# Expert weights read with two neighbouring matrix rows per partition in a two-layer hybrid trunk

## The chip, the cores and the metric

The kernel runs on one core of one Trainium2 chip. The core has a matrix engine (TensorE, PE in the profile, with its weight loads shown apart as PEld), a vector engine (VectorE, DVE), an engine for pointwise functions (ScalarE, ACT), GpSimd (POOL) and SyncE (SP). They run independently and wait for each other on semaphores. Data moves between the device's memory (HBM) and the on-chip memory (SBUF) through 16 DMA engines, which all queues share. The metric is device time in microseconds for the whole program, the median of the runs. All arithmetic is in 32-bit floats.

## What is computed

Two layers over 256 latent tokens and 256 context tokens, model width 1024. A layer is: modulation by a conditioning vector, three attention mixers with gates and an output projection, layer norm; then modulation again, a mixture of 16 experts in which each expert chooses its 32 tokens, and layer norm. The second layer leaves out the context tokens behind its attention, since only the latent stream is returned. What the change touches is the expert part:

```python
h = x * (1.0 + sc2) + sh2                   # modulation, one scale and shift per channel
y = expert_choice_ffn(h, w_router[l], w_gate[l], w_up[l], w_down[l])
x = layer_norm(ALPHA * x + g2 * y, ln2_g[l], ln2_b[l])

def expert_choice_ffn(h, w_router, w_gate, w_up, w_down):
    aff = jax.nn.softmax((h @ w_router).astype(jnp.float32), axis=-1)
    top_aff, top_idx = lax.top_k(jnp.swapaxes(aff, 1, 2), cap)          # cap = 32
    xs = h[bidx, flat].reshape(b, N_EXPERTS, cap, d)
    hid = jax.nn.silu(jnp.einsum('becd,edf->becf', xs, w_gate)) * jnp.einsum('becd,edf->becf', xs, w_up)
    ys = jnp.einsum('becf,efd->becd', hid, w_down) * top_aff[..., None].astype(h.dtype)
    return jnp.zeros_like(h).at[bidx, flat].add(ys.reshape(b, N_EXPERTS * cap, d))
```

`w_gate`, `w_up` and `w_down` are 1024 by 1024 matrices, one of each per expert and layer: 12 MB per expert, 192 MB per layer. They are read once, and each is used by 64 tokens in the first layer (32 of each stream) and by 32 in the second.

## The kernel before

The program is written out by hand, one instruction list per engine, and nothing reorders it. In each layer come: the input projection and attention (`qkv`, `attention`), the gates (`gates`), the output projection with the router (`project_and_route`), the choice of tokens (`choose`) and the experts (`experts`).

**How weights come in.** All weights of the program pass through one ring of 8 slots of 1 MB (`ring`, 128 partitions of 2048 floats each). The list `stream` holds them in the order in which PE uses them; SP goes through it and issues the load of piece n once the matmuls on piece n-8 are done (lines 836 to 868). So at most 8 pieces are on their way or waiting. The first four pieces of each layer's first expert have places of their own in `A` and `B` (`early_piece`) and are loaded once the gates are done. The modulation weights `w_ada` go through the same ring, as pieces of 128 rows of 2048 floats.

**How an expert matrix is cut.** `into(e)` takes `w_gate` and `w_up` in four pieces each, in turn, and `down(e)` takes `w_down` in four. A piece (number `kp`) is 256 rows of the matrix, 1 MB that lie together in HBM. It is loaded with the source view `"(k p) n -> p k n"`: partition p receives row 256 kp + p and row 256 kp + 128 + p, two runs of 4 KB. The matmul with contraction tile k then needs the 128 channels 128 k to 128 k + 127 of the tokens on its partitions.

**Who supplies the channels.** For gate and up, `gather(l, part)` on PE multiplies `X[:, tile, k * P:(k + 1) * P]` (128 channels as the stationary operand) with the one-hot choice of 4 experts; there are four such parts, part 0 ahead of the experts (in `choose`) and the others in `experts` behind `into(1)`, `into(2)` and `into(3)`. ACT (`gathered`) takes each result from PSUM into `xsT` and applies scale and shift there, from columns of `modcol`, one column for each 128 channels. For down, `turn_hidden(e)` transposes the columns `j * P:(j + 1) * P` of `hid`.

**An expert on PE**: `into(e)`; for e = 1 to 3 a gather; for e = 5, 9, 13 a scatter of four finished experts; `down(e - 1)`; `turn_hidden(e)`. With 64 tokens (first layer) a piece is four matmuls of 512 columns, with 32 tokens (second layer) eight of 256. The output rows of each expert are moved inside SBUF by four DMAs that POOL issues (`move_rows`, `B<-A` in the profile).

**The modulation columns.** `ada_rows(l)` transposes the finished `modcol` of a layer into a spare PSUM bank, ACT copies it to `mod_rows`, and POOL stores it. Its place in the first layer is in the attention, for the second layer in the first layer's experts (`ada_due`).

Of the kernel before, what the change touches and what calls it, by code (L numbers as in the profile page):

```python
# [17 lines left out]
P = 128  # L18
D = 1024
KT = D // P  # L20
DEPTH = 2
# [44 lines left out]
def trunk(nc, x, c, ctx_in, c_ctx, w_ada, b_ada, w_in, a_sink, b_q_norm, b_kv_norm, b_w_uq, b_w_ukv, c_q_norm,  # L66
          c_k_norm, w_branch, w_out, ln1_g, ln1_b, w_router, w_gate, w_up, w_down, ln2_g, ln2_b, consts, out):
    es = ExitStack()
    with es:
# [34 lines left out]
        bias_cols = sb("bias_cols", [P, 48 * DEPTH])  # L104
        modcol = sb("modcol", [P, DEPTH, 2, 48])
        mod_rows = sb("mod_rows", [96, P])
        wr = sb("wr", [P, KT, EXPERTS])
        sink = sb("sink", [P, HEADS_A])
        nsink = sb("nsink", [P, HEADS_A])
# [82 lines left out]
        bias_in = sem("bias_in")  # L192
        mod_stored = sem("mod_stored")
        mod_cols = sem("mod_cols")
        part_in = sem("part_in")
        parts = [0]
        early_in = [sem(f"early_in{i}") for i in range(4)]
# [57 lines left out]
        def second(eng, key):  # L255

            b, _, n = groups[key]
            eng.wait_ge(bank_drained[b], n - 1)
            return b

        def streams(l):
            return [0, 1] if l < DEPTH - 1 else [1]
# [87 lines left out]
        def _(pe):  # L350
# [84 lines left out]
            def ada_rows(l):  # L435
                pe.wait_ge(mod_cols, 3 * l + 3)
                b = begin(("adaR", l), bank=TURN_BANK)
                end(nc.tensor.transpose(psum[0:96, b, 0:P], modcol[:, l, :, :].rearrange("p s c -> p (s c)"), ident), b)

            def ada_hook(step):  # L440
# [256 lines left out]
            def gather(l, part):  # L697

                lo, w, per = gather_cut(l, part)
                for k0 in range(0, KT, per):  # L700
                    b = begin(("XS", l, part, k0))
                    at = 0
                    for k in range(k0, k0 + per):
                        for s in streams(l):
                            for i in (0, 1):
                                ins = mm(psum[:, b, at:at + w], X[:, 2 * s + i, k * P:(k + 1) * P],
                                         onehot[:, 2 * s + i, lo:lo + w], i == 0, i == 1)
                            at += w
                    end(ins, b)
# [16 lines left out]
            def experts(l):  # L726
# [4 lines left out]
                def into(e):  # L731
                    bg = begin(("HG", l, e))
                    bu = begin(("HU", l, e))
                    for part, (lo, _) in enumerate(GATHERS):
                        if e == lo:
                            for k0 in range(0, KT, gather_cut(l, part)[2]):
                                drained(pe, ("XS", l, part, k0))
                    for kp in range(4):
                        for at, (b, w) in enumerate(((bg, w_gate), (bu, w_up))):
                            src = [w[l, e, kp * 256:kp * 256 + 256, :]]  # L740
                            if e == 0 and kp < 2:
                                n, v = None, early_piece(l, 2 * kp + at, src, 2, D)
                            else:
                                n, v = piece(src, 2, D)
                            for k in (2 * kp, 2 * kp + 1):
                                for g in range(G):
                                    ins = mm(psum[g * M:(g + 1) * M, b, 0:Wd], xsT[:, k, e * M:(e + 1) * M],
                                             v[:, k % 2, g * Wd:(g + 1) * Wd], k == 0, k == KT - 1)
                            if kp == 3:
                                free(n, event=end(ins, b))  # L750
                            elif n is not None:
                                free(n, ins)

                def turn_hidden(e):
                    pe.wait_ge(hid_ready, EXPERTS * l + e + 1)
                    transposes(("HT", l, e), [hid[:, e % 2, j * P:(j + 1) * P] for j in range(Wd // P)])

                def down(e):
                    drained(pe, ("HT", l, e))
                    b = begin(("YE", l, e))  # L760
                    for kp in range(4):
                        n, v = piece([w_down[l, e, kp * 256:kp * 256 + 256, :]], 2, D)
                        for k in (2 * kp, 2 * kp + 1):
                            q, j = k // (Wd // P), k % (Wd // P)
                            for g in range(G):
# [69 lines left out]
        def _(sp):  # L835
            sp.dma_start(cst[:, :], consts).then_inc(consts_in, 16)

            for dst, src, n, after in stream:
                if after:

                    sp.wait_ge(*after)
                    sp.dma_start(dst, src[0].rearrange("(k p) n -> p k n", p=P)).then_inc(early_in[n], 16)
                    continue
                if n >= RING:
                    sp.wait_ge(*freed[n - RING])
# [95 lines left out]
        def _(act):  # L941
# [27 lines left out]
            def ada_hook(step):  # L969
# [3 lines left out]
                if "rows" in due:  # L973
                    b = filled(act, ("adaR", due["rows"]))
                    if due["rows"]:

                        act.wait_ge(mod_stored, 16 * due["rows"])
                    nc.scalar.copy(mod_rows[:, :], psum[0:96, b, 0:P]).then_inc(bank_drained[b], 1)

            def modulated(name, l, t, scale, shift, halves=(0,)):  # L980
# [146 lines left out]
            for l in range(DEPTH):  # L1127
# [43 lines left out]
                def gathered(part):  # L1171
                    lo, w, per = gather_cut(l, part)
                    n = len(streams(l))
                    for k0 in range(0, KT, per):
                        b = filled(act, ("XS", l, part, k0))
                        at = 0
                        for k in range(k0, k0 + per):
                            dst = xsT[:, k, n * lo:n * (lo + w)].rearrange("p (e m) -> p e m", m=M)
                            for i, s in enumerate(streams(l)):
                                ins = nc.scalar.activation(dst[:, :, CAP * i:CAP * i + CAP],  # L1180
                                                           psum[:, b, at:at + w].rearrange("p (e m) -> p e m", m=CAP),
                                                           ACT.Identity,
                                                           scale=modcol[:, l, s, 8 * SC2 + k:8 * SC2 + k + 1],
                                                           bias=modcol[:, l, s, 8 * SH2 + k:8 * SH2 + k + 1])
                                at += w
                        ins.then_inc(bank_drained[b], 1)

                if l == 0:
                    ada_hook("routed")
                gathered(0)  # L1190
                Wd = D * M // P
                for e in range(EXPERTS):
# [471 lines left out]
```

## Time and profile before

| | us |
|---|---|
| Median of 3 runs | 1913.62 (1913.56 to 1915.73) |
| Span of the profiled execution | 1912.5 |
| PE busy | 1559.2 (82%) |
| PE weight loads busy | 783.9 (41%) |
| DVE / ACT / POOL busy | 495.3 / 389.5 / 84.9 |
| Moved by DMA | 529.01 MB, mean 277 GB/s |

Times of the profile count from the span's start. The 40 slices of the page are 47.8 us each. The experts are on the engines from about 559 to 1090 us (first layer) and from about 1397 us to the end (second layer). The busy share of the DMA engines counts the time in which they held a packet, and can come out a little over 1. "SPq" is the time of SP's DMA-issuing instructions. A matmul of 32-bit floats stands in the profile as two records.

### The profile page before, as it was taken

What the parts mean: (1) busy time and instruction counts of PE and PEld (TensorE: products, weight loads), DVE (VectorE), ACT (ScalarE), POOL (GpSimd) and SP (SyncE); (2) the same over time, 40 slices, a digit from 0 to 9 for tenths busy, and PEclk for the clock granted to TensorE, in tenths of its full rate; (3) what the DMA queues carried; (4) which work ended last, traced back from release to release, by engine and by line L of the source; (5) the groups of instructions that cost most, each with busy time, mean ns of one, the idle gap of its engine ahead of it and who ended that gap; (6) DMA issues with size and microseconds to landing.
All of it is one profiled execution on the core that took longest, in us unless ns stands there. A gap on an engine that the chain in (4) does not pass through costs nothing.

```text
span 1912.5 us, 21336 instructions
## 1 busy us (share of the span) xinstructions
PE 1559.2 (82%) x8780; PEld 783.9 (41%) x8780; DVE 495.3 (26%) x1063; ACT 389.5 (20%) x877; POOL 84.9 (4%) x169
## 2 busy tenths in 40 slices
PE   5999999999979988778787799999866666666664
PEld 1544457888544522122222264578542322222221
DVE  0125775333440001010010344865320000000002
ACT  1313674222122200000000132753220000000000
POOL 1000000000000000000000010000000000000000
PEclk8999999999989999999999999999987767676767
DMA  9445713225258999999999721056769999999994
GB/s 377 154 171 245 289 40 99 98 86 186 109 204 340 396 394 400 393 403 392 403 400 391 275 65 39 1 159 214 286 238 401 406 402 405 402 406 402 406 402 184
DMA packets 151408, 529.01 MB, mean 277 GB/s; under 512 B 12800, under 2 KB 15120, under 8 KB 145168
## 3 DMA queue, kind: packets, MB, share of 16 engines
q1 hardware_dynamic: 143536, 510.44, 69.4%
q0 software_dynamic: 7232, 16.76, 2.8%
q8 instruction: 70, 1.15, 0.2%
q10 hardware_dynamic: 544, 0.45, 0.1%
q14 instruction: 26, 0.21, 0.0%
HBM read 520.17 MB, written 1.15 MB: 273 GB/s over the span
## 4 chain that ended last, share of the span: by engine, by line
PE 52%; DMA 37%; DVE 6%; SPq 4%; ACT 1%; issue 1%; ACTq 0%; POOL 0%; DVEq 0%
PE psum L412 48%; DMA ring<-in_w_up 17%; DMA ring<-in_w_down 15%; SPq L850 4%; PE psum L458 3%; DMA ring<-in_w_gate 2%; DMA ring<-in_w_in 2%; DVE small L1418 1%; DMA ring<-in_w_ada 1%; DVE PR L1438 1%; DVE X L1450 0%; DVE X L1449 0%; ACT hT L987 0%; DVE psum L1416 0%; DVE stats L1539 0%
## 5 line engine op out<-in xcount | busy, mean ns | idle before, releaser
L412 PE MATMUL psum<-ring,A 128*32 128x256 f32 (+2 forms) x4704 | 721.1, 547 | 254.6 <-DMA ring<-in_w_up 87.4
L412 PEld LDWEIGHTS psum<-ring,A 128*32 128x32 f32 (+2 forms) x4704 | 235.2, 139 | 713.4 <-issue 280.1
L412 PE MATMUL psum<-ring_r,h_hi 128*128 128x512 f32 x576 | 179.9, 394 | 5.8 <-DVE h_lo L1592 5.8
L1552 DVE TENSOR_TENSOR A<-A,psum 128x512 f32<-128x512 f32 (+1 forms) x32 | 17.7, 554 | 625.4 <-PE psum L412 625.4
L412 PE MATMUL psum<-ring,hT 128*128 128x512 f32 (+2 forms) x512 | 170.2, 486 | 10.7 <-DMA ring<-in_w_in 5.3
L412 PEld LDWEIGHTS psum<-ring_r,h_hi 128*128 128x128 f32 x576 | 109.5, 190 | 29.5 <-issue 6.6
L1199 ACT ACTIVATE A<-psum 128x512 f32<-128x512 f32 (+1 forms) x32 | 15.7, 491 | 519.0 <-PE psum L412 519.0
L412 PEld LDWEIGHTS psum<-ring,hT 128*128 128x128 f32 x512 | 85.6, 192 | 82.0 <-issue 79.2
L412 PE MATMUL psum<-ring_r,h_lo 128*128 128x512 f32 x288 | 113.1, 393 | 0.0
L346 POOL DMA_DIRECT2D B<-A x120 | 58.9, 497 | 951.2 <-DVE A L1568 950.2
L1592 DVE TENSOR_TENSOR ring_r<-ring,ring_r 128x2048 fp32r<-128x2048 f32 (+2 forms) x36 | 73.7, 2053 | 93.2 <-ACT ring_r L1118 93.0
L412 PE MATMUL psum<-A 128*128 128x512 f32 (+5 forms) x240 | 93.6, 526 | 3.6 <-ACT A L1180 3.6
L1568 DVE TENSOR_TENSOR A<-psum,PR 128x512 f32<-128x512 f32 (+1 forms) x32 | 17.9, 558 | 301.5 <-PE psum L412 301.5
L1118 ACT CAST ring_r<-ring 128x2048 fp32r<-128x2048 f32 (+2 forms) x36 | 61.9, 1719 | 133.8 <-DMA ring<-in_w_in 108.4
L1210 ACT COPY A<-psum 128x512 f32<-128x512 f32 (+1 forms) x32 | 15.4, 481 | 352.6 <-PE psum L458 352.6
L412 PE MATMUL psum<-ring,cs 128*32 128x512 f32 x384 | 54.9, 651 | 13.4 <-DMA ring<-in_w_ada 12.6
L1418 DVE TENSOR_REDUCE small<-psum 128x1 f32<-128x512 f32 (+1 forms) x96 | 57.4, 598 | 23.2 <-PE psum L412 22.2
L1083 ACT ACTIVATE PR<-psum,small 128x512 f32<-128x512 f32 (+1 forms) x96 | 58.7, 612 | 20.8 <-PE psum L412 7.1
L458 PEld LDWEIGHTS psum<-cst,PR 128*128 128x128 f32 x320 | 38.4, 142 | 52.3 <-DVE PR L1438 25.6
L412 PEld LDWEIGHTS psum<-ring_r,h_lo 128*128 128x128 f32 x288 | 54.8, 190 | 11.4
L412 PE MATMUL psum<-ring_r,o_hi 128*128 128x512 f32 x192 | 59.1, 389 | 0.0
L412 PE MATMUL psum<-B,hT 128*128 128x512 f32 x96 | 49.2, 667 | 9.6 <-DMA B<-A 9.6
(168 smaller groups left out, 1202.9 us busy)
## 6 DMA issues: line engine op xcount, KB each, us to landing
ring<-in_w_down SPq DMA_DIRECT2D x128, 1024.0 KB, 18.5
ring<-in_w_gate SPq DMA_DIRECT2D x124, 1024.0 KB, 18.7
ring<-in_w_up SPq DMA_DIRECT2D x124, 1024.0 KB, 19.1
ring<-in_w_ada SPq DMA_DIRECT2D x48, 1024.0 KB, 9.9
ring<-in_w_in SPq DMA_DIRECT2D x36, 1024.0 KB, 5.0
ring<-in_w_out SPq DMA_DIRECT2D x8, 1024.0 KB, 6.2
ring<-in_w_branch SPq DMA_DIRECT2D x8, 768.0 KB, 4.4
B<-A POOLq DMA_DIRECT2D x60, 64.0 KB, 5.8
```

The lines of the kernel that those rows point to most:

```text
L346: eng.dma_start(YG[CAP * (e % 4):CAP * (e % 4) + CAP, 2 * (g % 2) + s, n * Wd:(n + 1) * Wd], ysb[at:at + CAP, e % 2, 0:Wd]).then_inc(signa ...
L412: return nc.tensor.matmul(o, a, b, start=start, stop=stop, skip_group_check=True)
L458: ins = nc.tensor.transpose(psum[0:rows, b, i * P:(i + 1) * P], s, ident)
L850: sp.dma_start(dst, src[0].rearrange("(k p) n -> p k n", p=P)).then_inc(slot_filled[n % RING], 16)
L1083: nc.scalar.activation(prob[:, u % 4, 0:nk * P], psum[:, b, 0:nk * P], ACT.Exp, bias=small[:, c4:c4 + 1], scale=SCALE_B if br == "B" else ...
L1118: nc.scalar.copy(hi, src).then_inc(split_high, 1)
L1199: nc.scalar.activation(sil[:, e % 2, 0:Wd], psum[:, b, 0:Wd], ACT.Silu).then_inc(bank_drained[b], 1)
L1418: run(V_.tensor_reduce(small[:, c4 + 3:c4 + 4], psum[:, b, 0:nk * P], AX, ALU.max, negate=True))
L1438: V_.tensor_scalar(prob[:, u % 4, 0:nk * P], prob[:, u % 4, 0:nk * P], small[:, c4 + 2:c4 + 3], None, ALU.mult).then_inc(prob_ready, 1)
L1552: V_.tensor_tensor(hid[:, e % 2, 0:Wd], sil[:, e % 2, 0:Wd], psum[:, b, 0:Wd], ALU.mult) \
L1568: V_.tensor_tensor(ysb[:, (e - 1) % 2, 0:Wd], psum[:, b, 0:Wd], gate_y[:, 0:Wd], ALU.mult) \
L1592: V_.tensor_tensor(lo, src, hi_read, ALU.subtract).then_inc(split_low, 1)
```

## The change

A piece of an expert matrix is still the same 1 MB, but its source view is now `"(p j) n -> p j n"` with j = 2: partition p receives rows 256 kp + 2p and 256 kp + 2p + 1, which are neighbours in HBM. Both sides of the DMA are then one run of 8 KB per partition, 128 in all where there were 256 of 4 KB. Contraction tile k = 2 kp + j now stands for the 128 channels 256 kp + j, 256 kp + j + 2, and so on. To match, the stationary operand of the gather and that of the transposes of `hid` are read with a step of two floats (`pair_cols`), and the scale and shift columns that ACT applies must be in the permuted order: PE picks them out of `modcol` with four small matmuls per layer in `ada_rows`, ACT copies them to a new tile `modpair`, and `gathered` reads that.

```diff
+        modpair = sb("modpair", [P, DEPTH, 2, 2, KT])
+        def row_pairs(m):
+            return m.rearrange("(p j) n -> p j n", j=2)
+        def pair_cols(k):
+            return slice(256 * (k // 2) + k % 2, 256 * (k // 2) + 256, 2)
...
             def ada_rows(l):
                 pe.wait_ge(mod_cols, 3 * l + 3)
                 b = begin(("adaR", l), bank=TURN_BANK)
+                for j in (0, 1):
+                    for h in (0, 1):
+                        mm(psum[64 * h:64 * h + 64, b, P + j:P + 32:2], ident[:, j::2],
+                           modcol[:, l, :, 8 * SH2 + h:8 * SC2 + 8:2])
...
-                                ins = mm(psum[:, b, at:at + w], X[:, 2 * s + i, k * P:(k + 1) * P],
+                                ins = mm(psum[:, b, at:at + w], X[:, 2 * s + i, pair_cols(k)],
...
-                            src = [w[l, e, kp * 256:kp * 256 + 256, :]]
+                            src = row_pairs(w[l, e, kp * 256:kp * 256 + 256, :])
...
-                    transposes(("HT", l, e), [hid[:, e % 2, j * P:(j + 1) * P] for j in range(Wd // P)])
+                    transposes(("HT", l, e), [hid[:, e % 2, pair_cols(j)] for j in range(Wd // P)])
...
-                        n, v = piece([w_down[l, e, kp * 256:kp * 256 + 256, :]], 2, D)
+                        n, v = piece(row_pairs(w_down[l, e, kp * 256:kp * 256 + 256, :]), 2, D)
...
-                    sp.dma_start(dst, src[0].rearrange("(k p) n -> p k n", p=P)).then_inc(early_in[n], 16)
+                    sp.dma_start(dst, src).then_inc(early_in[n], 16)
...
+                    nc.scalar.copy(modpair[:, due["rows"], :, :, :],
+                                   psum[:, b, P:P + 32].rearrange("p (s w k) -> p s w k", s=2, w=2)) \
+                        .then_inc(modpair_ready, 1)
                     nc.scalar.copy(mod_rows[:, :], psum[0:96, b, 0:P]).then_inc(bank_drained[b], 1)
...
-                                                           scale=modcol[:, l, s, 8 * SC2 + k:8 * SC2 + k + 1],
-                                                           bias=modcol[:, l, s, 8 * SH2 + k:8 * SH2 + k + 1])
+                                                           scale=modpair[:, l, s, 1, k:k + 1],
+                                                           bias=modpair[:, l, s, 0, k:k + 1])
...
+                act.wait_ge(modpair_ready, l + 1)
                 gathered(0)
```

No instruction changes its place against the others. What is new on an engine's list stands at three places. On SP, where the first layer's expert loads begin (the shape is partitions by runs by floats; `in_w_ada` is a modulation piece), before:

```order
L847 DMA ring<-in_w_ada 128x2048 x4
L842 DMA A<-in_w_gate 128x2x1024
L842 DMA A<-in_w_up 128x2x1024
L842 DMA B<-in_w_gate 128x2x1024
L842 DMA B<-in_w_up 128x2x1024
L850 DMA ring<-in_w_gate 128x2x1024
```

and now:

```order
L861 DMA ring<-in_w_ada 128x2048 x4
L856 DMA A<-in_w_gate 128x2048
L856 DMA A<-in_w_up 128x2048
L856 DMA B<-in_w_gate 128x2048
L856 DMA B<-in_w_up 128x2048
L861 DMA ring<-in_w_gate 128x2048
```

The order is the same; an expert piece now has the form that a modulation piece had already, and so it is for all 384.

On PE, where `ada_rows(0)` stands in the first layer's attention (`modcol` are the modulation columns, `cst` the identity), before:

```order
L412 MATMUL psum<-A 128x256
L412 MATMUL psum<-ring,cs 32x512 x4
L412 MATMUL psum<-A 128x256
L438 MATMUL psum<-cst,modcol 96x128
L458 MATMUL psum<-cst,PR 128x128 x2
L412 MATMUL psum<-A 128x256
```

and now:

```order
L422 MATMUL psum<-A 128x256
L422 MATMUL psum<-ring,cs 32x512 x4
L422 MATMUL psum<-A 128x256
L422 MATMUL psum<-modcol,cst 64x16 x4
L452 MATMUL psum<-cst,modcol 96x128
L472 MATMUL psum<-cst,PR 128x128 x2
```

Four matmuls of 16 columns come in ahead of the transpose that was there.

On ACT at the same place, before:

```order
L1081 ACTIVATE small<-sink,small 128x1
L1083 ACTIVATE PR,small<-psum,small 128x256
L978 COPY mod_rows<-psum 96x128
L1097 COPY W<-psum 128x2x128
L1081 ACTIVATE small<-sink,small 128x1
```

and now:

```order
L1098 ACTIVATE small<-sink,small 128x1
L1100 ACTIVATE PR,small<-psum,small 128x256
L992 COPY modpair<-psum 128x32
L995 COPY mod_rows<-psum 96x128
L1114 COPY W<-psum 128x2x128
L1098 ACTIVATE small<-sink,small 128x1
```

One copy of 32 columns comes in ahead of the copy of `mod_rows`.

## Rows read from the trace of the kernel before

**Rows 1.** The page: GB/s moved in 40 slices; DMA packets by size
```profile
GB/s 377 154 171 245 289 40 99 98 86 186 109 204 340 396 394 400 393 403 392 403 400 391 275 65 39 1 159 214 286 238 401 406 402 405 402 406 402 406 402 184
DMA packets 151408, 529.01 MB, mean 277 GB/s; under 512 B 12800, under 2 KB 15120, under 8 KB 145168
```

**Rows 2.** Windows of both expert stretches: engines' busy us, clock, DMA share, GB/s
```profile
640.00:1070.00 430.00, 342.20 (x1461) 104.29 (x1457) 37.83 (x55) 22.16 (x44) 27.99 (x57) 1.00 1.03 397
1410.00:1890.00 480.00, 313.08 (x3127) 120.62 (x3116) 22.82 (x46) 22.13 (x58) 29.44 (x60) 0.72 1.01 398
```

**Rows 3.** Chain that ended last, first layer, then end: start, us, what
```profile
658.92 16.30 PE psum L412 x104
...
682.87 18.61 DMA ring<-in_w_down
...
1866.93 20.85 DMA ring<-in_w_down
```

**Rows 4.** PE's timeline at a second-layer expert: start, us, matmuls [idle before <-cause]
```profile
1605.00 1.94 PE L412 MATMUL psum<-ring,A 128*32 128x256 f32 x16 [0.62 <-DMA ring<-in_w_gate]
1607.57 1.93 PE L412 MATMUL psum<-ring,A 128*32 128x256 f32 x16 [0.63 <-DMA ring<-in_w_up]
1610.13 1.89 PE L412 MATMUL psum<-ring,A 128*32 128x256 f32 x16 [0.63 <-DMA ring<-in_w_gate]
```

**Rows 5.** Windows where the experts begin in the first layer, then in the second
```profile
565.00:570.00 5.00, 3.55 (x32) 3.36 (x31) 0.00 (x0) 4.42 (x12) 0.00 (x0) 1.00 0.03 13
...
575.00:580.00 5.00, 5.00 (x26) 2.07 (x24) 0.00 (x0) 0.00 (x0) 0.00 (x0) 1.00 0.00 0
580.00:585.00 5.00, 5.00 (x28) 2.15 (x24) 0.60 (x1) 0.67 (x2) 0.00 (x0) 1.00 0.93 315
...
1400.00:1405.00 5.00, 3.20 (x39) 2.80 (x41) 0.00 (x0) 4.25 (x9) 0.00 (x0) 0.98 0.00 0
```

**Rows 6.** Windows with 8 KB runs (modulation pieces), then with 4 KB runs (expert pieces)
```profile
142.00:154.00 12.00, 12.00 (x40) 5.23 (x39) 2.40 (x6) 1.81 (x5) 0.00 (x0) 1.00 1.00 421
192.00:206.00 14.00, 13.88 (x92) 7.01 (x92) 10.94 (x47) 10.32 (x39) 0.00 (x0) 1.00 1.01 420
...
625.00:635.00 10.00, 10.00 (x71) 6.62 (x68) 0.69 (x1) 3.51 (x9) 0.00 (x0) 1.00 1.03 412
1445.00:1455.00 10.00, 6.58 (x68) 2.14 (x64) 0.00 (x0) 0.38 (x1) 0.00 (x0) 0.68 1.03 410
```

**Rows 7.** DMA rate in 40 slices of 640 to 1070 us, then of 1410 to 1890 us
```profile
GB/s 395 389 408 379 400 410 380 409 410 373 402 409 371 410 410 374 410 409 383 407 409 400 381 409 371 409 407 383 410 408 370 410 410 399 380 409 372 407 410 373
```
```profile
GB/s 400 409 394 410 408 394 410 394 408 410 396 410 409 393 410 394 410 407 395 409 401 403 408 396 410 408 395 409 397 408 409 396 408 409 395 409 394 410 409 180
```

**Rows 8.** SP's issues as the first layer's expert loads begin: start, us of issuing
```profile
579.18 0.37 SPq L850 DMA_DIRECT2D ring<-in_w_gate  x1
...
600.56 0.37 SPq L850 DMA_DIRECT2D ring<-in_w_up  x1
609.77 0.37 SPq L850 DMA_DIRECT2D ring<-in_w_gate  x1
```

**Rows 9.** PE's timeline, first layer: a gather, a scatter, four transposes, pieces of an expert
```profile
586.57 13.95 PE L412 MATMUL psum<-ring,A 128*64 128x512 f32 x64
600.45 7.41 PE L412 MATMUL psum<-W,X 128*128 128x128 f32 x64
...
859.50 3.60 PE L412 MATMUL psum<-B,hT 128*128 128x512 f32 x8
863.03 7.09 PE L412 MATMUL psum<-ring,A 128*64 128x512 f32 x32
870.05 0.66 PE L458 MATMUL psum<-cst,A 128*128 128x128 f32 x4
```

**Rows 10.** Rows nearest to what is added: 16-column matmuls, a transpose, a copy
```profile
1383.86 3.59 PE L412 MATMUL psum<-wr,hT 128*128 128x16 f32 x16 [0.75 <-ACT hT L987]
...
181.28 0.27 PE L438 MATMUL psum<-cst,modcol 128*96 128x128 f32 x1
...
184.68 0.24 ACT L978 COPY mod_rows<-psum 96x128 f32<-96x128 f32 x1
```

More of the change, by code:

```diff
@@ L194, in trunk @@
         mod_cols = sem("mod_cols")
+        modpair_ready = sem("modpair_ready")
         part_in = sem("part_in")
```

## The prediction, made before the changed kernel ran

> **What bounds the kernel now.** I read the slices of the page first [rows 1]: the DMA rate is flat at about 390 to 405 GB/s in two stretches, slices 13 to 22 and 31 to 39, and far lower elsewhere. These are the experts of the two layers. Then the windows over them [rows 2]: the DMA engines' busy share is 1.03 and 1.01, while PE is busy for 342 of 430 us in the first and 313 of 480 in the second. Then the chain that ended last [rows 3]: in the experts it alternates between short runs of PE and waits of 18 to 21 us for a ring load. Such a wait is not the time of one load; it is eight loads in a queue. PE's timeline says the same [rows 4]: one piece every 2.56 us, matmuls of 1.9 us on it, then idle until the next piece lands. So inside the experts the time is the number of pieces times the DMA engines' time for one, and outside them the change touches almost nothing.
>
> Where does the queue begin to bind? Not at the first expert load. In the first layer the DMA engines stand still from 565 to about 581 us [rows 5]: four early pieces and eight ring pieces have landed, and nothing can be issued until PE has freed a slot, which happens at 579.18 [rows 8]. In the second layer they are likewise idle at 1400 to 1405 [rows 5]. What was loaded before those gaps is hidden, whatever its rate. A layer has 16 x 12 = 192 pieces; less 4 early and 8 in the ring, 180 remain behind the gap. Both layers: 360 pieces, 377.5 MB, on the path to the end.
>
> **Part 1: the run length.** The trace already holds loads of 8 KB runs: the modulation weights are 1 MB pieces of the very form that an expert piece now gets. Where several of them follow each other, with nothing beside them, the rate is 421 GB/s over 12 us and 420 over 14 us. Expert pieces with 4 KB runs, in windows without a move of output rows, give 410 and 412 [rows 6]. The best slices of both expert stretches also stop at 408 to 410, over and over [rows 7], so 410 is the plateau of 4 KB runs and the 412 is the edge of a short window. Per piece of 1.0486 MB: 2.557 us at 410 (PE's rhythm of 2.56 agrees [rows 4]), 2.491 us at 421. Saved: 0.067 us, and 360 x 0.067 = **24 us**. With the other pair, 412 against 420, it is 0.049 us and 17.5 us. I take 24, since the 410 rests on many slices and the 421 on a row without other traffic, and keep 17 as the low end. The high end has no row for experts; it comes with the moves, below.
>
> **Part 2: what stays around it.** Every expert has a dip in the rate where POOL moves output rows inside SBUF, down to 370 to 380 GB/s in a slice of the first layer and 394 in the second [rows 7]. Against 410 the first window loses 430 x (1 - 397/410) = 13.6 us over some 13 experts, so about 16 us in the layer; the second loses 480 x (1 - 398/410) = 14 us, of which 6.7 belong to its last slice (12 us at 180), so about 7. In all some 23 us are lost around the moves. The moves' own packets don't change, the packets they queue among do: half as many, twice as long. No row shows 8 KB runs beside a move. I take the loss as unchanged, and keep both ends: gone (-23) and doubled (+23).
>
> **Part 3: does something else bind first?** PE. In the first layer a piece takes it 13.95/8 = 1.74 us with no wait [rows 9], 12 pieces 20.9 us, transposes 0.66, a scatter 3.6 in one expert of four, against 12 x 2.49 = 29.9 us of loads. With a gather: 20.9 + 0.6 + 7.4 = 28.9, still below. In the second layer 12 x 1.93 = 23.2 us at the low clock. So PE keeps behind the loads, and the gain is not given back there. The tight spot is the first refill: SP issues twelve pieces from 579.18 to 600.56 and the next only at 609.77, when PE is through with a gather [rows 8]. Twelve pieces last from about 581 to 581 + 30.7 = 611.7 before and to 610.9 now; a new issue needs about 2 us to move data (579.18 against 581). So the queue was just not dry and may now be for up to 1 us. **+0.5**.
>
> **Part 4: the strided reads.** The gather's stationary operand and that of the transposes of hid are read at a step of two floats. A gather is 64 records in 7.41 us [rows 9], 0.116 us each, so its pace is that of weight loads as much as of 128-column matmuls; no row of this trace has a stationary operand with a step. If reading every second float costs nothing, 0; if it doubles the load, see the rivals. I take 0, the value of the nearest row, the same load without a step; the other end is priced among the rivals. The SBUF — State Buffer page of the Trainium skill ("Door 1: The DMA port swizzle", note on cachelines) says memory is read in lines of 16 bytes and that two hits per line keep full bandwidth, which a step of two floats just meets. No row here shows it.
>
> **Part 5: the columns.** Per layer four small matmuls on PE and one ACT copy. The nearest rows: sixteen records of 16 columns in 3.59 us at the low clock, 0.22 each, so eight records 1.8 us; and a transpose of 128 columns in 0.27 us, which at the high clock bounds four matmuls by 1.1 us [rows 10]. The copy is like that of mod_rows, 0.24 us. In the second layer's case they lie among the first layer's experts and are hidden by waits for loads. In the first they stand in the attention, where PE leaves gaps of 0.4 to 0.9 us per unit to DVE and ACT: between 0 and 2 us. **+0.5**. ACT's new wait for modpair stands before gathered(0); in both layers the copy is hundreds of microseconds old by then. Nothing queues behind it.
>
> Sum: 1913.6 - 24 + 0.5 + 0.5 = 1890.6, rounded to **1890**. The profiled execution lies at a span of 1912.5, 1.1 under the median; the sum is of differences, so I set it against the median.
>
> **Rivals.**
> - *The moves cost less* beside packets of 8 KB: up to 23 us more gain, 1867. For it: the dip is larger than the moves' bytes ask for (64 KB x 4 is 0.6 us of 410 GB/s, the dip in the first layer is 1 us on top of that), so something per packet is lost there, and weights bring half as many packets. Against it: it may be the moves' own packets that cost.
> - *The moves cost more*: each of their packets waits behind one of 8 KB, twice as long. Doubled loss: 1890 + 23 = 1913, no change.
> - *The rate goes by bytes, not by run length*: the 421 is owed to PE and DVE doing other work then, or to the modulation matrix's row pitch. Then every piece takes 2.557 us still, and the two additions stay: 1914.6. Against it are four windows that differ by run length and agree with each other [rows 6]. The DMA: Bandwidth & Descriptors page of the Trainium skill ("Specifications") speaks for this rival: it puts the threshold for line rate at 512 B, which 4 KB runs passed long ago. By it the sum would be 1914.6, by the rows 1890; the trace disagrees with the page as far as 410 against 421 goes.
> - *Slower: weight loads with a step*. Place: gathers of both layers, from part 0 on. At twice the time of a load a gather in the first layer takes 14.8 us: part 0 starts the experts 7.4 us later, parts 1 to 3 bring PE to 36.3 us per expert against 31.4 of loads with a move, 3 x 4.9 = 14.7; the second layer's part 0 is half as long, 3.7. Together 26: 1890 + 26 = 1916, no change. That is the point from which it decides; at three times it is 14.8 + 3 x 12.3 + 7.4 = 59, so 1949.
>
> **How the numbers follow.** Forecast (1879 to 1900, where parts 1, 3 and 5 vary and the moves' loss by a third): 0.72. Moves cheaper or a better rate than 421 (1862 to 1879): 0.10. Moves dearer: 0.06, half of it under 1909. By bytes: 0.05. Loads with a step: 0.07, of which 0.03 near 1916 and 0.04 beyond. About 0.2% (3.8 us) is what a measurement of this kernel can tell from no change. Faster: 0.72 + 0.10 + 0.03 = 0.85 and 0.01 of partial cases, 0.86; within 0.2%: 0.03 + 0.04 + 0.03 = 0.09 with rounding; slower: 0.05. Range: from 1874, a third of the way into the first rival, to 1903, which leaves out the rivals without change and the slower ones.
>
> **What would show it.** The page would count 49,152 packets fewer, 102,256, with those under 8 KB down to 46,864 (from 145,168 [rows 1]), or the runs were not joined. Slices in the experts without a move: 420 to 422 GB/s; if they stay at 410, the rate goes by bytes. Slices with a move: some 10 above today's 373 and 394; higher or lower tells the moves' share. PE's rhythm in the second layer 2.49 us. A gather 7.4 us, else the step costs. The span from the first issue behind the gap to the last landing in each layer shorter by 12 us, and everything ahead of 560 us and behind the last piece the same within 2 us. The prediction is wrong if the experts shorten by less than 15 us or more than 35, or if the attention grows.

## The result, and the profile after

| | before | after |
|---|---|---|
| First measurement, median | 1914.56 us (1913.56 to 1915.73, 4 runs) | 1892.93 us (1888.70 to 1896.54, 4 runs) |
| Ratio, 95% interval | | 0.9889 (0.9873 to 0.9905) |
| Measured again with the experiments | 1914.07 us (23 runs) | 1892.10 us (1891.08 to 1893.46, 4 runs), ratio 0.988 (0.9867 to 0.9892) |
| Span of the profiled execution | 1912.5 us | 1886.7 us |

The changed kernel is 22 us faster, 1.1 to 1.2%. The profiled execution of it is the fastest of the four, at the lower edge of their spread, so its span is 26 us shorter and not 22.

The page of the changed kernel, slices and packets (of before: [rows 1]):

```profile
GB/s 379 159 165 242 307 40 91 95 94 173 134 206 306 396 402 410 402 410 405 405 410 402 297 66 40 1 141 207 282 232 412 416 412 416 412 416 413 416 412 192
DMA packets 102256, 529.01 MB, mean 280 GB/s; under 512 B 12800, under 2 KB 15120, under 8 KB 46864
```

49,152 packets fewer for the same bytes: two runs of 4 KB have become one of 8 KB in all 384 expert pieces. (A run is a stretch of bytes that lies together on both sides of the DMA.) In the slices that hold experts alone, 15 to 22 and 31 to 39, the rate is 402 to 416 GB/s where it was 391 to 406; in the others it moves both ways, since the slices of the shorter span don't begin at the same work. For a like comparison, both kernels in the same two windows inside the experts, with the columns of [rows 2]. Before:

```profile
640.00:1050.00 410.00, 328.07 (x1401) 100.39 (x1397) 36.48 (x54) 21.57 (x43) 26.03 (x53) 1.00 1.03 397
1430.00:1850.00 420.00, 273.47 (x2664) 102.55 (x2668) 20.97 (x41) 16.24 (x43) 27.47 (x56) 0.71 1.03 404
```

After:

```profile
640.00:1050.00 410.00, 341.60 (x1439) 107.69 (x1435) 37.83 (x55) 22.31 (x45) 27.25 (x56) 0.98 1.01 406
1430.00:1850.00 420.00, 274.65 (x2738) 104.90 (x2731) 20.99 (x41) 16.22 (x43) 25.48 (x52) 0.73 1.01 414
```

And the same windows of the changed kernel in 40 slices each (of before: [rows 7], in slightly wider windows):

```profile
GB/s 378 410 422 376 420 421 381 421 420 379 413 418 374 422 422 376 422 422 372 420 422 421 366 422 401 398 420 413 382 422 418 369 422 422 380 422 422 373 422 421
...
GB/s 420 420 400 423 418 400 421 421 401 421 424 398 424 417 404 419 421 402 420 419 401 420 422 400 424 419 402 420 422 401 423 414 405 423 408 412 420 406 416 420
```

Where the plateau, the rate of the best slices over and over, stood at 410 it stands at 421 to 422. But in the first layer the dips, one for each expert, still go down to 366 to 382, so they are deeper by about as much as the plateau has risen.

PE's timeline at a second-layer expert of the changed kernel (of before: [rows 4]):

```profile
1589.27 1.94 PE L422 MATMUL psum<-ring,A 128*32 128x256 f32 x16 [0.55 <-DMA ring<-in_w_up]
1591.76 1.58 PE L422 MATMUL psum<-ring,A 128*32 128x256 f32 x16 [0.56 <-DMA ring<-in_w_gate]
1594.24 1.07 PE L422 MATMUL psum<-ring,A 128*32 128x256 f32 x16 [0.90 <-DMA ring<-in_w_up]
```

A piece every 2.49 us where it was every 2.56, and PE still idles for it. The two profiles by stretches, in us, the experts of a layer taken from the first matmul of the first expert to the start of the last piece of the last one:

| stretch | before | after | |
|---|---|---|---|
| ahead of the first layer's experts | 570.35 | 566.58 | -3.8 |
| first layer's experts | 499.75 | 490.90 | -8.9 |
| between | 333.9 | 333.4 | -0.5 |
| second layer's experts | 483.83 | 471.17 | -12.7 |
| from the last piece on | 24.7 | 24.6 | -0.1 |

The stretch ahead is not the change's: in the profiles of the eight further kernels below whose gathers have no step of four, the first expert starts anywhere between 567.3 and 570.5.

### The profile page after: what moved, and what is told of

Read it like the earlier page. It is cut to its first block, busy times and chain, and to the rows that moved or that the text cites. A ratio compares the mean times of both kernels' runs of the same rounds, so it can differ in the third digit from the quotient of the medians.

```text
span 1886.7 us, 21372 instructions
## 1 busy us (share of the span) xinstructions
PE 1557.4 (83%) x8796; PEld 788.5 (42%) x8796; DVE 495.3 (26%) x1063; ACT 389.5 (21%) x879; POOL 84.8 (4%) x169
## 4 chain that ended last, share of the span: by engine, by line
PE 51%; DMA 41%; DVE 6%; ACT 1%; issue 1%; ACTq 0%; POOL 0%; DVEq 0%
PE psum L422 48%; DMA ring<-in_w_up 24%; DMA ring<-in_w_down 14%; PE psum L472 3%; DMA ring<-in_w_in 2%; DVE small L1436 1%; DVE PR L1456 1%; DVE X L1468 0%; DVE X L1467 0%; ACT hT L1004 0%; DVE psum L1434 0%; DMA ring<-in_w_ada 0%; DVE stats L1557 0%; DVE X L1552 0%; DMA PR<-in_c 0%
```

## The experiments

All diffs are against the changed kernel, except in the last experiment.

**The theory (R)**: each run in a DMA has a fixed cost besides its bytes (theory F in the later texts is this with its price, 0.072 us a MB for 128 runs); the loads bind in the experts; so halving the number of runs is the whole gain, and the permutation that it needs is nearly free. Rivals: the gain comes from where the rows lie in HBM (H); the step in the weight loads gives back much of it (W).

### The changed kernel once more

> The changed kernel once more, for its spread and as the measure of the runs beside it. Theory R (the gain comes from the length of a run in the DMA; the step in the weight loads and the columns cost next to nothing): 0.989 of the kernel before, as measured. No rival says otherwise; what is to be seen is whether its single times again lie apart by 8 us, where those of the kernel before lie within 2.

Measured: 1892.10 us, 1891.08 to 1893.46, and the kernel before now lies between 1911.48 and 1917.91 in 23 runs. Its four times lie within 2.4 us of each other now, and those of the kernel before within 6.4. So the 8 us between the first four times are no trait of the changed kernel, and single times differ by several us in either; what follows is compared by medians, and a difference of 1 to 2 us between two medians of four runs is not to be told from none.

### One half of the change alone: the loads

```diff
-                                ins = mm(psum[:, b, at:at + w], X[:, 2 * s + i, pair_cols(k)],
+                                ins = mm(psum[:, b, at:at + w], X[:, 2 * s + i, k * P:(k + 1) * P],
...
-                    transposes(("HT", l, e), [hid[:, e % 2, pair_cols(j)] for j in range(Wd // P)])
+                    transposes(("HT", l, e), [hid[:, e % 2, j * P:(j + 1) * P] for j in range(Wd // P)])
```

(also without the small matmuls and the copy, with `modcol` in `gathered`.)

> The loads of the changed kernel, 8 KB runs, with the compute of the kernel before: channels, scales and transposes in the old order, no small matmuls, no copy. The products are those of mismatched rows, so the output is not the reference's; every instruction that it has costs what it would. Theory R: 0 to 2 us below the changed kernel, since the step in the weight loads showed 7.80 us a gather against 7.41 and stands on the path only in part 0 of either layer. Rival W (weight loads with a step cost much of the gain): 5 us or more below the changed kernel. If the changed kernel's spread is owed to the step, this one's times lie close together.

Measured: 1892.95 us (1891.24 to 1896.69), ratio 0.9886 (0.9873 to 0.99), against 1892.10 for the changed kernel beside it. The loads alone bring all of the gain. It was expected at or up to 2 us under the changed kernel and came 0.9 above, which is within the scatter; rival W, 5 us or more below, is out.

### The other half alone: the step and the columns

```diff
-                            src = row_pairs(w[l, e, kp * 256:kp * 256 + 256, :])
+                            src = [w[l, e, kp * 256:kp * 256 + 256, :]]
```

(the same for `w_down`, and the old view at the early pieces.)

> The other half alone: the loads of the kernel before (two runs of 4 KB), with the compute of the changed kernel. Again mismatched rows, so the output is not the reference's. Theory R: 0 to +2 us against the kernel before (1914 to 1917). Rival W: +5 or more. Windows without a move in the experts at 410 GB/s.

Measured: 1913.65 us (1911.62 to 1916.10, 11 runs), ratio 0.9995 (0.9987 to 1.0004). The permutation costs nothing that can be measured in the time. It does cost PE something. Gathers of this kernel, PE's timeline, first layer:

```profile
599.91 7.80 PE L422 MATMUL psum<-W,X 128*128 128x128 f32 x64
629.66 7.80 PE L422 MATMUL psum<-W,X 128*128 128x128 f32 x64
```

7.80 us where it was 7.41 [rows 9]: 5% for the step of two floats, on an engine that mostly waits for loads here anyway.

### Same places in HBM, short runs

```diff
-                    sp.dma_start(dst, src).then_inc(slot_filled[n % RING], 16)
+                    sp.dma_start(dst[:, ::-1, :] if len(dst.shape) == 3 else dst, src).then_inc(slot_filled[n % RING], 16)
...
-                                             v[:, k % 2, g * Wd:(g + 1) * Wd], k == 0, k == KT - 1)
+                                             v[:, 1 - k % 2, g * Wd:(g + 1) * Wd], k == 0, k == KT - 1)
```

> The changed kernel, but with the two rows of a pair written to the ring slot in swapped order, and read so by the matmuls. The bytes come from HBM in the same places, two neighbouring rows to one partition, but the write side is two runs of 4 KB in the wrong order, so the DMA has 256 pieces of 4 KB again. Theory R: the windows without a move go back to 410 GB/s and the time to that of the kernel before, 1914 to 1917. Rival H (the gain comes from neighbouring rows being read together in HBM, not from the length of a piece): 420 GB/s, the time of the changed kernel, 1891 to 1894.

Measured: 1916.00 us (1912.99 to 1918.34, 12 runs), ratio 1.0009 (1.0000 to 1.0018). Its packets, which are as many as in the kernel before, then the slices of its DMA rate, 640 to 1050 us:

```profile
DMA packets 151408, 529.01 MB, mean 277 GB/s; under 512 B 12800, under 2 KB 15120, under 8 KB 145168
...
GB/s 381 402 409 386 392 410 374 410 409 410 377 408 388 391 410 406 374 410 410 370 410 410 367 403 409 368 410 408 384 400 410 399 378 410 409 368 409 410 367 409
```

The plateau is back at 410. H is out: neighbouring rows read together bring nothing as long as they are written as two runs. Against the changed kernel this differs in the length of a run and in the order in which a pair lies in its slot. The order by itself shows no cost, since the plateau is that of the kernel before, whose two runs lie in plain order. So the run length is worth 1916.0 - 1892.1 = 23.9 us, with what the moves of output rows do beside it.

### Runs of 2 KB

```diff
+                    if len(dst.shape) == 3:
+                        dst = dst.rearrange("p j (h n) -> p (j h) n", h=2)[:, ::-1, :]
+                        src = src.rearrange("p j (h n) -> p (j h) n", h=2)
                     sp.dma_start(dst, src).then_inc(slot_filled[n % RING], 16)
```

> The changed kernel with each expert piece written to its slot in four parts of 512 floats in reversed order, so that the DMA has 512 runs of 2 KB; the matmuls read as before, so the output is not the reference's. Theory F: 256 runs more than the 4 KB form, 2.557 + 0.144 = 2.70 us a MB, a plateau of 388 GB/s and 52 us more than the kernel before, 1966. If cost per run grows only under some length, it lies elsewhere.

Measured: 1965.42 us (1961.93 to 1965.71), ratio 1.0259 (1.0243 to 1.0274). Its packets, 98,304 more than in the kernel before (256 for each of 384 pieces), its windows as above, then its slices of the first:

```profile
DMA packets 249712, 529.01 MB, mean 269 GB/s; under 512 B 12800, under 2 KB 15120, under 8 KB 243472
...
640.00:1050.00 410.00, 315.21 (x1347) 98.59 (x1343) 35.74 (x52) 20.54 (x42) 24.01 (x49) 1.00 1.05 378
1430.00:1850.00 420.00, 292.62 (x2670) 113.39 (x2666) 17.36 (x35) 20.20 (x53) 23.52 (x48) 0.62 1.04 378
...
GB/s 387 360 387 387 363 387 387 361 387 387 374 371 386 373 368 386 387 360 387 387 357 386 387 387 355 387 387 354 387 386 354 387 387 381 366 387 387 358 387 387
```

Theory F gave 388 and 1966; 387 and 1965 came. The cost goes with the number of runs, and one is as dear at this length as at twice it.

### Four neighbouring rows, 16 KB runs

```diff
+            return m.rearrange("(p j) n -> p j n", j=4)
...
+            return slice(512 * (k // 4) + k % 4, 512 * (k // 4) + 512, 4)
...
+                        mm(psum[32 * h:32 * h + 32, b, P + j:P + 32:4], ident[:, j::4],
+                           modcol[:, l, :, 8 * SH2 + h:8 * SC2 + 8:4])
...
+                            src = row_quads(w[l, e, kq * 512:kq * 512 + 512, :])
...
+                                n, v = double_piece(src)
```

> The change taken one step further, with the full computation: four neighbouring rows per partition, 16 KB runs, 2 MB to a DMA and two ring slots, for gate, up and the first layer's down (the second layer's down keeps pairs); channels are taken at a step of four. If each run carries a fixed cost, the plateau goes 410, 422 and then 428: per MB 2.557, 2.485, 2.449 us, 0.036 us for each of 300 MB behind the gaps, 10 to 12 us less than the changed kernel, 1880 to 1882. If the plateau is a ceiling already reached with 8 KB, it stays at 422 and the time at 1892 or some us above, since a slot pair is refilled more coarsely. Rival: reading stationary operands at a step of four floats costs PE more than the step of two; then the gathers grow beyond 8 us and the first layer begins later.

Measured: 1921.23 us (1919.50 to 1923.07), ratio 1.0039 (1.0026 to 1.0051): slower than the kernel before. PE's timeline of it shows why:

```profile
558.81 15.20 PE L442 MATMUL psum<-W,X 128*128 128x128 f32 x64 [1.25 <-DVE W L1560]
...
605.95 15.20 PE L442 MATMUL psum<-W,X 128*128 128x128 f32 x64
621.08 7.09 PE L442 MATMUL psum<-ring,A 128*64 128x512 f32 x32
...
643.10 15.20 PE L442 MATMUL psum<-W,X 128*128 128x128 f32 x64
```

A gather takes 15.20 us, not 7.80, as the rival in the text above had it. The two changes lie over each other here, so the next two take them apart.

### The step of four alone

```diff
-                                ins = mm(psum[:, b, at:at + w], X[:, 2 * s + i, pair_cols(k)],
+                                ins = mm(psum[:, b, at:at + w], X[:, 2 * s + i, slice(512 * (k // 4) + k % 4, 512 * (k // 4) + 512, 4)],
```

(and the transposes of `hid` at a step of four.)

> The changed kernel with the stationary operands of the gathers and of the transposes of hid read at a step of four floats and not two; loads as in the changed kernel, so the output is not the reference's. A gather was 7.41 us without a step and 7.80 with two. Theory R (no path through PE but part 0): a gather of 7.8 to 8.2 us and the same time, 1892 to 1894. Rival S (each read of another 16 bytes costs): a gather of 12 to 15 us, part 0 and the first refills late, 1905 to 1920.

Measured: 1920.27 us (1919.92 to 1920.50, 5 runs), ratio 1.0033 (1.002 to 1.0046), 28 us above the changed kernel. Theory R missed here: it had expected no more from a step of four than from one of two. Rival S had the kind right; 15.20 us and 1920.3 lie at the top of its ranges. Windows of 10 us over the first experts show PE busy throughout, and the loads starved in some (the first of them holds the start of the refill, the last two are plain):

```profile
580.00:590.00 10.00, 10.00 (x50) 4.09 (x47) 0.47 (x1) 0.60 (x1) 0.00 (x0) 1.00 0.46 156
590.00:600.00 10.00, 10.00 (x57) 4.45 (x57) 0.22 (x1) 2.54 (x5) 0.00 (x0) 1.00 1.01 413
...
610.00:620.00 10.00, 10.00 (x45) 10.00 (x44) 0.00 (x0) 4.17 (x12) 0.00 (x0) 1.00 0.64 268
620.00:630.00 10.00, 10.00 (x50) 4.27 (x51) 1.12 (x4) 2.09 (x5) 1.13 (x3) 1.00 0.61 220
```

Its PE weight loads of the gathers and of the transposes, by form (busy us, mean ns of one), then the same two rows of the kernel before, without a step:

```profile
L422 PEld LDWEIGHTS psum<-W,X 128*128 128x128 f32 x384 | 90.2, 329 | 7.2 <-issue 4.9 <-DVE W L1530 2.3
L472 PEld LDWEIGHTS psum<-cst,A 128*128 128x128 f32 x144 | 19.5, 186 | 22.1 <-issue 20.9 <-DVEq L1248 0.9
...
L412 PEld LDWEIGHTS psum<-W,X 128*128 128x128 f32 x384 | 48.4, 210 | 6.4 <-issue 4.1 <-DVE W L1512 2.3
L458 PEld LDWEIGHTS psum<-cst,A 128*128 128x128 f32 x144 | 15.9, 146 | 22.1 <-issue 20.9 <-DVEq L1230 0.9
```

In the changed kernel the first of these rows reads 51.0 us and 215 ns, the second 19.4 and 186. So the gather's weight loads pay little for a step of two and much for one of four, and those of the transposes pay for a step of two, 146 to 186 ns, and nothing more for four. A third of the 144 are other transposes, which were not changed; inside the first layer's experts (640 to 1050 us), where all are those of `hid`, it is 140, 208 and 209 ns, and for the gather 192, 196 and 329. What holds for a gather of the first layer, then: 7.41 us without a step, 7.80 at two floats, 15.20 at four. Where the 28 us lie, by the stretches of the table above (one profile each): 8.9 us more ahead of the first expert, 18.4 in the first layer's experts, 2.7 between the layers' experts and 1.9 in the second layer's.

### 16 KB runs without a step

The kernel with 16 KB runs, with `k * P:(k + 1) * P` and `j * P:(j + 1) * P` at the two places.

> The loads of the 16 KB runs with the stationary operands read without a step, so that rows and channels do not match and the output is not the reference's. It parts the two effects that lay over each other: a gather of 15.20 us and the longer runs. Theory F (a fixed cost per run, 0.072 us a MB for 128 runs fewer, so 0.036 us more for the next halving): plateau 428 GB/s, 10 to 12 us under the changed kernel, 1881. Rival C (8 KB already at the ceiling, or the 2 MB pieces give back what they gain, since a slot pair comes free later and in larger steps): 1890 to 1896.

Measured: 1893.09 us (1892.23 to 1893.70), ratio 0.9884 (0.9868 to 0.9901). Windows and slices as for the others (in the second layer, whose `w_down` keeps its 8 KB runs, two pieces of three are of the new form):

```profile
640.00:1050.00 410.00, 336.62 (x1471) 114.53 (x1471) 37.11 (x54) 23.23 (x48) 25.97 (x53) 0.96 1.01 406
1430.00:1850.00 420.00, 255.88 (x2750) 116.26 (x2754) 20.97 (x41) 16.21 (x43) 25.47 (x52) 0.78 1.01 415
...
GB/s 379 380 428 425 363 427 407 386 430 432 363 428 420 379 430 424 370 433 427 362 427 420 404 398 425 369 427 427 358 424 430 373 418 424 421 366 420 396 408 425
```

Both theories hold in part. The plateau rises to 425 to 430, as the fixed cost says; the average stays at 406 and 415, where the changed kernel had 406 and 414. The dips go deeper, most of them to 358 to 373, and eat it. The time is in rival C's range. Part of that may be the coarser ring, since a slot pair comes free only with its last matmul: early in the first layer a window of 5 us has the DMA engines busy for 0.92 of it:

```profile
590.00:595.00 5.00, 5.00 (x26) 1.72 (x24) 0.00 (x0) 0.00 (x0) 0.00 (x0) 1.00 0.92 347
```

Over the whole window from 640 to 1050 that share is 1.01, as in the changed kernel, so such moments are few there. How much of the loss is the ring's and how much the moves' stays open. A full version with 16 KB runs would need the channels in `X` regrouped before the gather, to be free of the step of four; at 1893 before that cost there was nothing to win by it.

### The moves of output rows cut down

Each move carries one row instead of 32:

```diff
-                    eng.dma_start(YG[CAP * (e % 4):CAP * (e % 4) + CAP, 2 * (g % 2) + s, n * Wd:(n + 1) * Wd],
-                                  ysb[at:at + CAP, e % 2, 0:Wd]).then_inc(signal, 16)
+                    eng.dma_start(YG[CAP * (e % 4):CAP * (e % 4) + 1, 2 * (g % 2) + s, n * Wd:(n + 1) * Wd],
+                                  ysb[at:at + 1, e % 2, 0:Wd]).then_inc(signal, 16)
```

In the kernel before:

> The kernel before, but each DMA that moves output rows inside SBUF (four per expert) carries one row instead of 32; the other rows are left as they were, so the output is not the reference's. All waits stay. Bytes taken out: 6.1 MB, about 15 us at 410 GB/s. In the kernel before, the windows of the experts average 397 and 404 GB/s against a plateau of 410, a loss of some 13 of 410 us and 6 of 420, 21 us over both layers. Theory M (that loss is the moves'): 15 + 21 = 36 us less than the kernel before, 1878. If the dips come from something else, 15 us less, 1899.

and in the changed kernel:

> The same cut in the changed kernel. There the windows average 406 and 414 against a plateau of 422, a loss of 15.5 of 410 us and 8.0 of 420, 27 us over both layers, 6 more than before. Theory M: 15 + 27 = 42 us less than the changed kernel, 1850, so that the change alone, without moves, is worth 28 us and the moves take 6 of it back. Rival: the moves cost the same beside either run length, then 36 us less, 1856, and the change is worth 22 without them too.

Measured: 1877.53 us (1876.66 to 1880.23) and 1853.86 us (1851.39 to 1855.64); ratios 0.9813 (0.9800 to 0.9827) and 0.9686 (0.9673 to 0.9700). Their slices of the DMA rate, 640 to 1050 us, first the kernel before without moves:

```profile
GB/s 408 410 408 409 409 409 410 409 409 409 410 408 409 408 409 408 410 409 408 408 409 409 408 410 409 410 408 409 410 409 407 409 410 408 409 410 408 410 409 299
```

then the changed kernel without moves (its experts end at about 1037 us):

```profile
GB/s 421 420 420 420 421 422 420 420 422 420 421 420 421 422 419 423 422 418 421 421 420 420 422 420 422 420 421 422 420 420 422 422 417 423 421 419 422 422 335 215
```

With the moves cut to one row there are no dips, in either. The 31 rows that each move leaves out cost 1914.0 - 1877.5 = 36.5 us before (36 was expected) and 1892.1 - 1853.9 = 38.2 us after (42 and 36 were expected), of which 15 are their bytes (estimated: 6.1 MB at 410 GB/s). Without them the run length is worth 23.7 us, with them 22.0. For both numbers the text above had two values, 42 and 28 if the moves take back some of the gain and 36 and 22 if they don't; the medians lie between and can't decide it. The stretches of the experts, free of what varies ahead of them, say more (us in one profile each, both layers together, by the marks of the table above):

| | with moves | cut to one row | |
|---|---|---|---|
| loads of 4 KB runs | 983.6 | 949.8 | -33.8 |
| loads of 8 KB runs | 962.1 | 924.3 | -37.8 |
| difference | -21.5 | -25.5 | |

The other profiles with the same loads and whole moves lie near: 983.5 and 985.2 (the step alone, the swapped pairs), 962.8 and 961.8 (the changed kernel again, the loads alone). So within the experts the longer runs are worth some 25 us, and the moves take about 4 of it back.

## Why the prediction was right, and where it was off

1890 was predicted, 1892.9 and 1892.1 were measured: a gain of 23 us was expected and one of 22 came. That it came so near is partly luck, since part 1 was 2 us too small and part 2, held at nothing, was 2 to 5 us too small the other way. By its own parts:

**What binds, and from where.** Right. The experts' two stretches shortened, the 334 us between them did not, and nor did the end. The 360 pieces behind the gaps carry the effect.

**Part 1, the run length: 24 us.** The mechanism is shown. The size was a little off. In the kernels with the moves cut the slices average 409 (4 KB runs, the first 39) and 421 (8 KB runs, the first 38); a piece of 2^20 bytes takes 2.564 and 2.492 us at these, 0.072 less and not 0.067: 26 us over 360 pieces, where 1 GB/s more or less in either rate is 2 us. The experts' stretches without moves gave 25.5. The 23.9 us of the swapped pairs is less since it holds what the moves take. That the modulation pieces, loaded earlier in the same program, could stand for expert pieces to come was the useful step: their rows said 421 and 420 [rows 6].

**Part 2, the moves: unchanged.** This is the part that was wrong: the loss grew, by 2 to 5 us. By the windows, the loss against the plateau was 410 x (1 - 397/410) = 13.0 us and 420 x (1 - 404/410) = 6.1 us before, and is 410 x (1 - 406/422) = 15.5 us and 420 x (1 - 414/422) = 8.0 us after, about a quarter more; with the 23 us over both layers whole that the prediction had, that makes 28. The other run lengths fit in the first layer's window: 9.5 us at 2 KB (378 of 387), and some 21 at 16 KB (406 of 428, the ring's share in it). The experts' stretches with and without moves say 4.0 us more, and the medians (36.5 and 38.2 us) 1.7, which is no more than their own scatter. So the rival of dearer moves was right in kind, at a tenth to a fifth of the 23 us that I had set as its end. Whether it works as the rival says, each packet of a move waiting behind a longer one, no run shows.

**Part 3, the first refill: +0.5.** SP's issues in the changed kernel (of before: [rows 8]), then windows of it:

```profile
596.84 0.33 SPq L861 DMA_DIRECT2D ring<-in_w_up  x1
606.44 0.33 SPq L861 DMA_DIRECT2D ring<-in_w_gate  x1
...
600.00:605.00 5.00, 5.00 (x43) 4.59 (x43) 0.00 (x0) 3.85 (x12) 0.00 (x0) 1.00 1.01 423
605.00:610.00 5.00, 5.00 (x26) 1.66 (x24) 0.00 (x0) 1.07 (x4) 0.00 (x0) 1.00 0.97 374
```

The queue did run dry for a moment, for some 5 x (1 - 374/423) = 0.6 us by the rates (an estimate).

**Part 4, the strided reads: 0.** Right for the time, wrong for the instruction: 0.39 us more for each of the first layer's four gathers. (Those of the second layer can't be compared: the granted clock over them was 1.00 in the kernel before and 0.83 to 0.88 in the changed one.) The profile of the loads alone has 489.2 us for the first layer's experts against 490.9 with the step, but the medians of the two kernels don't differ by more than their scatter. The rule of the Trainium skill that I had cited (SBUF — State Buffer, "Door 1: The DMA port swizzle", lines of 16 bytes, two hits per line keep the rate) can now be held against rows: at a step of two floats, which is two hits, 7.80 for 7.41; at four, one hit, 15.20. For the gather the measurements agree with it in the main, though two hits still cost 5%. For the transposes of `hid` they don't: their group of loads goes from 146 ns without a step to 186 at two floats, where the rule has no cost, and stays at 186 at four, where it has one.

**Part 5, the columns: +0.5.** The matmuls took 0.42 us and the copy 0.18 (PE's timeline, first layer, and the groups of `modpair` in the changed kernel):

```profile
180.31 0.42 PE L422 MATMUL psum<-modcol,cst 128*64 128x16 f32 x8
...
L992 ACT COPY modpair<-psum x2: 172/179/186, 183.6 to 642.6; 128x32 f32<-128x32 f32 x2
```

In the kernel with the step and the columns alone nothing of it can be seen in the time. The 1.0 us of parts 3 and 5 together is below what these runs can tell.

**The rivals.** "By bytes, not by run length" fell with the 422 and once more with the swapped pairs. The rule of the DMA: Bandwidth & Descriptors page of the Trainium skill that went with it ("Specifications", line rate from 512 B on) does not hold as a plateau here: 387, 410, 422 and some 428 GB/s at 2, 4, 8 and 16 KB. "Weight loads with a step" did not occur at two floats but is real: at four, the doubled gather that it had priced at 26 us cost 28, by the path that it had named (7.4 us at the start, 14.7 in the first layer's experts and 3.7 in the second layer's gather were priced; 8.9, 18.4 and, with the second layer's experts, 4.6 are in the profile).

## What to carry to other kernels

Where one queue of large loads binds, look for another tensor in the same trace that already has the access pattern in question: here its rate gave the gain within 2 us, where the rule of a threshold gave none. Count the runs of a DMA, not only its bytes; when contraction rows can be permuted freely, neighbouring rows on one partition make the runs longer, and the price lies in how the other operand is then read: a step of two floats was nearly free for the gather, a step of four doubled it. A plateau that rises does not lift the dips beside it; take the average of a window, and know what the dips are made of.

## What the runs showed of the hardware

- A run in one of these loads costs about 9 ns on its DMA engine besides its bytes (an estimate from the rates). Rows that are neighbours in HBM but go to SBUF as two runs count as two: 410 GB/s. Worked out from the plateaus: a piece of 2^20 bytes takes 2.710, 2.557, 2.485 and 2.450 us at 387, 410, 422 and 428 GB/s, with 32, 16, 8 and 4 runs on each of 16 engines; the differences are 0.153 us for 16 runs, 0.072 for 8 and 0.035 for 4, which is 9.6, 9.0 and 8.8 ns each. Rates read to 1 GB/s leave about 1 ns open in the first two; the last rests on a plateau of 425 to 430, and can be anything from 4 to 12.
- DMAs inside SBUF beside the loads cost more than twice their bytes: 6.1 MB, 15 us of the plateau's rate, took 36.5 us beside 4 KB runs and 38.2 beside 8 KB runs (33.8 and 37.8 by the experts' stretches alone).
- A weight load of 128 columns of 32-bit floats for a matmul, read at a step of four floats, took 329 ns in the mean against 215 at a step of two and 210 at none (329, 196 and 192 inside the first layer's experts, at a granted clock of 0.98 to 1.00), and a gather made of them 15.20, 7.80 and 7.41 us. Transposes behave otherwise: 140 ns without a step, 208 at two floats and 209 at four in the same window.
